# Attention within a tile: the causal mask taken from TensorE and given to VectorE and GpSimd

## The reference

```python
def fox_block(q, k, v, Fq, Fk, qpos, kpos):
    s = einsum('bqhd,bkhd->bhqk', q, k) * FOX_HEAD_DIM ** -0.5
    s = s + (Fq[..., :, None] - Fk[..., None, :])          # forget gate, moved to (head, query, key)
    s = where(kpos[None, :] <= qpos[:, None], s, -inf)
    p = softmax(s, axis=-1)
    return einsum('bhqk,bkhd->bqhd', p, v)
```

## Time and profile before

| what | value |
|---|---|
| median of 3 runs | 3674.41 us (3671.79 to 3679.04) |
| the profiled execution | 3677.2 us, span of its trace 3675.5 us |
| PE busy | 3058.5 us, 83% |
| DVE busy | 2164.2 us, 59% |
| ACT busy | 1057.2 us, 29% |
| POOL busy | 1440.1 us, 39% |
| mean granted clock of TensorE | 0.963 of 2.4 GHz |
| first block | up to about 850 us |

### The profile page before, as it was taken

The page is one execution under the profiler, slowest core; times in us unless marked ns, Lnnn a source line. Parts: engine busy times, 40 slices in busy tenths (PEclk is TensorE's granted clock), DMA queues, the critical chain, the costliest instruction groups (busy, mean ns, idle before and its releaser), DMA issues.

```text
span 3675.5 us, 29378 instructions
## 1 busy us (share of the span) xinstructions
PE 3058.5 (83%) x9023; PEld 1415.7 (39%) x9023; DVE 2164.2 (59%) x5158; ACT 1057.2 (29%) x3284; POOL 1440.1 (39%) x1185
## 2 busy tenths in 40 slices
PE   6899999997768977987897788788878878887776
PEld 2566666665213333332332333233333333332222
DVE  0343444434885775686577558657855865785444
ACT  1122222223323233223322322332232233223222
POOL 0000000001444555555555454545545554555553
PEclk7789999999879999999999999999999999999999
DMA  9300000032999999999999999999999999999998
GB/s 342 126 20 30 29 23 21 21 118 98 422 373 422 421 421 418 421 421 416 416 421 416 412 422 414 418 421 417 416 410 422 421 416 412 421 419 421 421 418 349
DMA packets 196495, 1219.15 MB, mean 332 GB/s; under 512 B 35696, under 2 KB 36656, under 8 KB 55792
## 3 DMA queue, kind: packets, MB, share of 16 engines
q0 software_dynamic: 156672, 1140.92, 75.1%
q1 hardware_dynamic: 39664, 76.34, 5.8%
HBM read 1205.68 MB, written 11.50 MB: 331 GB/s over the span
## 4 chain that ended last, share of the span: by engine, by line
DMA 45%; PE 8%; DVE 8%; issue 7%; ACT 5%; POOL 4%; POOLq 0%
DMA shared<-in_uv,eidx_even 23%; DMA shared<-in_uv,eidx_odd 22%; PE bank L942 8%; DVE shared L1244 5%; POOL shared L907 4%; ACT wt L1042 2%; ACT dg L1046 2%; ACT ge L1039 1%; PE bank L954 0%; DVE ti L1127 0%; DVE shared L1162 0%; DVE shared L1159 0%; DVE shared L1129 0%; DVE bp L1127 0%; DVE e L1164 0%
## 5 line engine op out<-in xcount | busy, mean ns | idle before, releaser
L942 PE MATMUL bank<-shared,dg 128*128 128x512 f32 (+1 forms) x4352 | 2002.8, 623 | 527.9 <-ACT dg L1046 527.8
L942 PEld LDWEIGHTS bank<-shared,dg 128*128 128x128 f32 (+1 forms) x4352 | 768.4, 191 | 1753.7 <-ACT dg L1046 952.4
L907 POOL DMA_INDIRECT shared<-in_uv,eidx_even x576 | 738.4, 1282 | 769.9 <-PE bank L942 638.0
L1244 DVE CUSTOM_DVE_ANT_0 shared<-shared,h_even 128x1024 f32<-128x1024 f32 x576 | 702.1, 1222 | 502.3 <-DMA shared<-in_uv,eidx_even 501.2
L907 POOL DMA_INDIRECT shared<-in_uv,eidx_odd x512 | 654.8, 1279 | 638.1 <-PE bank L942 554.7
L1244 DVE CUSTOM_DVE_ANT_0 shared<-shared,h_odd 128x1024 f32<-128x1024 f32 x512 | 625.2, 1222 | 420.8 <-DMA shared<-in_uv,eidx_odd 419.7
L1039 ACT ACTIVATE ge<-dots 128x2 f32<-128x2 f32 x544 | 110.6, 203 | 1878.3 <-DVE dots L1244 1878.2
L1046 ACT ACTIVATE dg<-ident,wt 128x128 f32<-128x128 f32 x1024 | 355.3, 394 | 16.7
L929 PE MATMUL bank<-wk,h2T 128*128 128x512 f32 x512 | 260.5, 595 | 0.0
L370 PE MATMUL bank<-shared,hT 128*128 128x512 f32 (+3 forms) x576 | 221.5, 546 | 0.0
L283 POOL TENSOR_SCALAR qr<-qs 128x8 f32<-128x8 f32 (+1 forms) x9 | 1.8, 196 | 409.7 <-DVE qs L695 409.7
(11 more groups left out here) (286 smaller groups left out, 2051.3 us busy)
## 6 DMA issues: line engine op xcount, KB each, us to landing
wout<-in_w_ada SPq DMA_DIRECT2D x12, 2048.0 KB, 9.0
shared<-in_w_in SPq DMA_DIRECT2D x1, 10288.0 KB, 33.2
shared<-in_uv,eidx_even POOLq DMA_INDIRECT x576, 12.5
shared<-in_uv,eidx_odd POOLq DMA_INDIRECT x512, 12.5
wout<-in_w_out SPq DMA_DIRECT2D x1, 4096.0 KB, 31.3
xn<-in_x_prompt SPq DMA_DIRECT2D x8, 512.0 KB, 5.4
xt<-in_x_prompt SPq DMA_DIRECT2D x8, 512.0 KB, 4.7
xmid<-mix SPq DMA_DIRECT2D x8, 512.0 KB, 3.1
```

The lines of the kernel that those rows point to most:

```text
L907: pool.indirect_dma_start(ring[:, k % RING, :], None, a["uv"], bass.IndirectOffsetOnAxis(flat(eidxs[n % 2][:, :, :])[:, k:k + 1], 0)).then ...
L942: mm = pe.matmul(bank[SUM_BANK(n) + c][at:at + T, :], dg[:, k % RING, 0:T], ring[:, k % RING, DM + 512 * c:DM + 512 * c + 512], start=(k = ...
L1244: ins = dve.tensor_tensor_reduce(ring[:, sl, 0:DM], ring[:, sl, 0:DM], h2s[n % 2][:, :], 1.0, 0.0, ALU.mult, ALU.add, dots[:, k:k + 1])
```

## The change

The two mask matmuls go. For the maximum, DVE adds `maskq` to the own scores of all four heads in one tensor_tensor into the first half of `mix`, and reduces from there. Since `mix` is written earlier in the tile than before, DVE waits there for the store of the last tile's xmid. For the weights, the exponential is taken of unmasked own scores, and GpSimd sets the entries with key > query to zero in place (`affine_select`), once per head, after the exponential and before PE's weighting with the own keys. PE waits for that with a new semaphore `own_masked`. GpSimd's queue is now: power for q and k, power for v, select of head 0, of head 1, power for the next x, select of head 2, power for y, select of head 3.

```diff
--- before.py
+++ after.py
@@ -177,6 +177,7 @@
             HB = lambda n: (HIST(n) + 3) // 4
             HIST_BEFORE = lambda n: sum(FH * HB(m) for m in range(n))
             KEYS_BEFORE = lambda n: sum(FH * (HB(m) + 1) for m in range(n))
+            own_probs = lambda h, T: (pT[0:T, 8, 0:T], pown[0:T, 0:T])[h % 2]
             KEY_BANK = lambda n, h, c: 5 + h % 3 if HB(n) == 0 else 6 - c if HB(n) == 1 else 5 + (c + 1) % 3
 
             @block.sync
@@ -283,14 +284,26 @@
                     then(pool.tensor_scalar(out, src, 1.0 / mean_of, EPS, ALU.mult, ALU.add))
                     pool.tensor_tensor(out, out, mhalf[0:out.shape[0], 0:out.shape[1]], ALU.pow).then_inc(sem(done), 1)
 
+                def own_masked(n, h):
+
+
+                    T = T_OF(n)
+                    pool.wait_ge(sem("pT_exp"), KEYS_BEFORE(n) + (HB(n) + 1) * (h + 1))
+                    pool.affine_select(out=own_probs(h, T), in_=own_probs(h, T), pattern=[[1, T]], compare_op=ALU.is_ge, fill=0.0,
+                                       base=0, channel_multiplier=-1).then_inc(sem("own_masked"), 1)
+
                 power(rstd[0:TS, :], ssum[0:TS, :], DM, "x_sq", 0, "rstd")
                 for n in range(NT + 1):
                     T = T_OF(n)
                     power(qr[0:T, :], qs[0:T, :], FD, "qk_sum", n, "qk_rstd")
                     power(vr[0:T, :], var[0:T, :], 64, "v_var", n, "v_rstd")
+                    own_masked(n, 0)
+                    own_masked(n, 1)
                     if n < NT:
                         power(rstd[:, :], ssum[:, :], DM, "x_sq", n + 1, "rstd")
+                    own_masked(n, 2)
                     power(yr[0:T, :], ysum[0:T, :], SI, "y_sq", n, "y_rstd")
+                    own_masked(n, 3)
 
             @block.tensor
             def _(pe):
@@ -403,8 +416,7 @@
                     if not FIRST(n):
                         pe.wait_ge(sem("hist_kept"), n)
                     for h in range(FH):
-                        pe.matmul(bank[2][0:T, h * P:h * P + T], qT[0:AUG, h, 0:T], kc[0:AUG, h, 0:T], start=True, stop=False)
-                        mm = pe.matmul(bank[2][0:T, h * P:h * P + T], ident[0:T, 0:T], maskq[0:T, 0:T], start=False, stop=True)
+                        mm = pe.matmul(bank[2][0:T, h * P:h * P + T], qT[0:AUG, h, 0:T], kc[0:AUG, h, 0:T], start=True, stop=True)
                     mm.then_inc(sem("own_scores"), 1)
                     pe.wait_ge(sem("um_gelu"), n + 1)
                     pe.wait_ge(sem("sums_used"), n + 1)
@@ -445,8 +457,7 @@
                                     mm = pe.matmul(bank[bk][:, j * P:j * P + T], kh[0:AUG, h, (4 * c + j) * P:(4 * c + j + 1) * P], qT[0:AUG, h, 0:T],
                                                    start=True, stop=True)
                             else:
-                                pe.matmul(bank[bk][0:T, 0:T], kc[0:AUG, h, 0:T], qT[0:AUG, h, 0:T], start=True, stop=False)
-                                mm = pe.matmul(bank[bk][0:T, 0:T], maskq[0:T, 0:T], ident[0:T, 0:T], start=False, stop=True)
+                                mm = pe.matmul(bank[bk][0:T, 0:T], kc[0:AUG, h, 0:T], qT[0:AUG, h, 0:T], start=True, stop=True)
                             mm.then_inc(sem("key_scores"), 1)
 
                     def weigh(h):
@@ -454,6 +465,7 @@
                         probs, own = ((pT, pT[:, 8, :]), (pT2, pown))[h % 2]
                         for j in range(HT):
                             pe.matmul(bank[2][0:T, h * 65:h * 65 + 65], probs[:, j, 0:T], vh[:, j, h, :], start=(j == 0), stop=False)
+                        pe.wait_ge(sem("own_masked"), n * FH + h + 1)
                         pe.matmul(bank[2][0:T, h * 65:h * 65 + 65], own[0:T, 0:T], vt[0:T, h, :], start=(HT == 0), stop=True).then_inc(sem("pv"), 1)
 
                     by_key(0)
@@ -571,7 +583,7 @@
                                 w = min(4, HT - 4 * c)
                                 ins = act.activation((pT, pT2)[h % 2][:, 4 * c:4 * c + w, 0:T], bank[bk][:, :].rearrange("p (j n) -> p j n", j=4)[:, 0:w, 0:T], ACT.Exp)
                             else:
-                                ins = act.activation((pT[0:T, 8, 0:T], pown[0:T, 0:T])[h % 2], bank[bk][0:T, 0:T], ACT.Exp)
+                                ins = act.activation(own_probs(h, T), bank[bk][0:T, 0:T], ACT.Exp)
                             ins.then_inc(sem("pT_exp"), 1)
                         if h == 1 and not last:
                             act.wait_ge(sem("x_in"), 16 * n + 32)
@@ -729,7 +741,10 @@
                     ins.then_inc(sem("M"), 1)
 
                     dve.wait_ge(sem("own_scores"), n + 1)
-                    then(dve.tensor_reduce(mh[0:T, :, 0], bank[2][0:T, :].rearrange("p (h n) -> p h n", h=FH)[:, :, 0:T], X, ALU.max))
+                    prev(dve, sem("xmid_stored"), n * 16)
+                    own4 = mix[0:T, 0:512].rearrange("p (h n) -> p h n", h=FH)[:, :, 0:T]
+                    then(dve.tensor_tensor(own4, bank[2][0:T, :].rearrange("p (h n) -> p h n", h=FH)[:, :, 0:T], bc(maskq[0:T, 0:T].rearrange("p (h n) -> p h n", h=1), [T, FH, T]), ALU.add))
+                    then(dve.tensor_reduce(mh[0:T, :, 0], own4, X, ALU.max))
                     for h in range(FH):
                         for c in range(HB(n)):
                             i = h * HB(n) + c
```

## The result

The changed kernel takes 3696.76 us (median of 5, 3691.31 to 3699.35) against 3674.41 us before (3671.79 to 3679.04): ratio 1.0055, 95% interval 1.0043 to 1.0068. It is slower by 0.55% (22 us between the medians, 20 between the profiled executions), and outside the forecast range. The profiled execution took 3697.26 us with a span of 3695.5 us.

The account below looks back on a forecast made before the run. The second block's gathers end last, so only its start, set by the first block, can move. Tile 0 -2.5, tile 1 +0.1, tiles 2 and 3 +1.5, tiles 4 to 8 +0.3: -0.6 us, giving 3673.8 us, range 3667 to 3682.

Parts of the forecast that it names:

- What bounds the kernel: Second block's gathers end last, untouched; the change moves only the first block, where DVE is late at the own scores.
- The add: Own scores, tiles 2 to 8: DVE's mask add costs 0.72 us per tile on the path, +5.0 us in all.
- PE would be 0.9 us earlier, but only waits longer for DVE: worth nothing.: Own scores, tiles 2 to 8: removing four PE mask pairs (0.9 us) gains nothing, since DVE is late.
- vanish in that wait: net 0: Own scores, tile 1: removed masks vanish in PE's 0.75 us wait for DVE's products; the add has room; net 0.
- Tile 0: First tile, partly at the 1.2 GHz level: own masks -1.3 us, by-key masks -1.2 us, together -2.5 us.
- By key, tiles 4 to 8: Scores by key: three exposed mask pairs leave PE's path, -0.66 us per tile, -3.3 in all; GpSimd's select is covered.
- Tiles 1 to 3, priced at nothing: Scores by key: the removed 0.66 us runs into PE's wait for vn, worth 0; later vn adds +0.2 us in all.
- the row of the power operation: GpSimd's power on 128x4 did not stretch beside DVE, so no contention was priced; by the contention rule about +1 us instead.
- Rival (a): GpSimd becomes the late one, with selects up to 1.65 us: +8.7 us, 3682 us in all; chance 0.06.
- Rival (c): Tile 0's clock shifts because PE's passes change: 3664 or 3684 us; chance 0.08, half to each side.
- Either sign: Clock shifts from changed PE passes could gain or lose: 10 us for 20 us of PE work at the other level.

Follow-up runs that it names:

- kernel with four pairs: Whole change plus four mask-sized matmul pairs per tile that compute nothing, behind the own scores; against the kernel before: 3669.05 us, ratio 0.9992.
- without own masks: Kernel before with PE's four own-score masks left out and nothing in their place (maximum over unmasked scores): 3690.79 us, ratio 1.0043.
- the add alone: Kernel before with DVE's mask add put in and all PE masks kept: 3684.09 us, ratio 1.0025.
- own-score half: Kernel before with DVE adding the own-score mask instead of PE; scores by key still masked by PE, no GpSimd select: 3699.39 us, ratio 1.0066.
- G: Theory, not a run: PE's wider waits between own scores and scan products make its granted clock fall behind them, and that is the loss.
- by-key half alone: Kernel before with only the GpSimd select replacing PE's masks by key; own scores masked by PE, no DVE add: 3669.32 us, ratio 0.9985.
- changed kernel with the gap filled: Whole change plus six idle matmul pairs behind the second history score, in tiles with history; against the kernel before: 3677.44 us, ratio 1.0006.
- the one with both places filled: Whole change plus idle matmul pairs behind the own scores and behind history scores; against the kernel before: 3668.19 us, ratio 0.9983.
- filled by-key half: Kernel before with only the by-key masks moved to GpSimd, plus one to four idle matmul pairs at PE's other waits: 3672.51 us, ratio 0.9992.

## Why the prediction was wrong

**What bounds the kernel** was read rightly: only the first block moved, and DVE, not PE, was the late one at the own scores.

**The add** was right at +0.72 us and on the path (11.12 against 10.40 us in tile 5 of the kernel with four pairs). Its row came out at 0.68 us for a forecast 0.67 to 0.69.

**"PE would be 0.9 us earlier, but only waits longer for DVE: worth nothing."** This is the step that failed. The wait was seen, and sized, and priced at zero because PE is not the late engine there. At a held clock the price of zero was right (10.40 us in tile 5 with the masks and without). But a PE that waits wasn't free here: the clock that it got afterwards went with the wait, and what stands behind the wait (later history scores, scan products) is on the path. The removed masks and the added DVE work both widened the same wait, from 0.9 to 2.5 us in tile 2 and from nothing to 1.7 us in tile 5. The masks' removal alone costs 16 us (without own masks), the add alone 10 us (5 of it its own term), both together 24 us (own-score half). Each is mostly the clock.

**Tile 1's masks "vanish in that wait: net 0"** failed in the same way. Its wait for the products grew from 0.75 us to 1.64, and the clock fell; the tile grew by 1.9 us. In all five profiled kernels with a wait of 1.64 to 1.68 us there the clock falls during it or within 2 us of its end, in none of the eight with 0.75 us or less.

**Tile 0** was -5.8 us for -2.5, and the profiles of the halves part it. From the mark to the first scores by key it took 12.77 us before and 9.54 after, -3.2 for a forecast of -1.3. All six profiled kernels whose PE masks the own scores take 12.7 to 12.9 us there and have a fall that begins 0.7 to 1.6 us behind the mark; six of the seven others take 8.8 to 9.5 without it, the seventh 10.4 with one. From there to the mark of tile 1 it is 74.8 us in all five kernels with the masks by key and 72.2 to 72.3 in seven of the eight without, -2.6 for a forecast of -1.2. Before the change, then after it:

```profile
170.50:177.00 6.50, 6.50 (x14) 2.31 (x14) 2.58 (x6) 0.00 (x0) 0.00 (x0) 0.50 0.00 0
...
166.50:177.00 10.50, 8.68 (x46) 4.07 (x44) 9.34 (x21) 0.63 (x2) 1.20 (x2) 1.00 0.00 1
```

The sum mis-sized both terms because it took the low clock as given. With the clock held the own masks are worth nothing there too: the kernel with four pairs takes the same 9.54 us. Why the early fall goes with the masks isn't shown, and G doesn't explain it: the change widens PE's wait there from nothing to 1.33 us, and the clock gets better.

**By key, tiles 4 to 8** was right: -0.67 in tile 5. In tile 8 it was more, 14.40 for 15.23 us, since there the first mask pair was exposed as well. Tiles 1 to 3, priced at nothing, were shorter by 0.1 to 0.2 us each in the kernel with four pairs. The by-key half alone was to bring 4.3 us and brought some 5.5 (0.9985). It may have a price of its own: of the seven profiled kernels that have this half and no pairs in front of the wait for vn, five lose the clock in tile 2 at the scores by key or behind them, some 2.6 us each where it could be compared; of the five that mask by key on PE, none does. No run was made to test that.

**GpSimd.** The select took 0.29 us as forecast where nothing else was going on, but not always: over the profiled execution it had a median of 292 ns and a maximum of 785 (ns min/median/max, then first and last start):

```profile
L292 POOL TENSOR_SCALAR_AFFINE_SELECT pown<-pown x18: 232/292/785, 179.9 to 841.1; 128x128 f32<-128x128 f32 x16, 64x64 f32<-64x64 f32 x2
...
340.48 0.44 PE L469 MATMUL bank<-vt,pown 128*128 128x65 f32 x2 [0.51 <-POOL pown L292]
```

All ten above 0.31 us in this execution overlap DVE instructions on SBUF, as the 0.57 us one overlaps L633 above. Not every such overlap stretched one: the select at 573.21 took 0.29 us beside a product of two SBUF tensors. The prediction held the row of the power operation against the rule of the Trainium skill (GPSIMD Engine Reference, "Key points") that GpSimd contends with DVE for SBUF; here the stretched selects agree with the rule and the row misled, probably since that operation hardly reads anything. It cost little: PE waited for a select four times, all in tiles 1 and 2, 1.8 us together (0.60 us the longest), and PE waits for vn behind it anyway. Rival (a) did not come about; in the by-key half alone its whole price is inside a gain.

**Rival (c)** named the clock, gave it 0.08, and looked for it in tile 0, where it had been low already. I read the clock where it had fallen, and not the waits behind which it might fall next. "Either sign" was the other fault: in tiles 1 to 8 the change widens PE's waits in front of the scan products and narrows none of them, and there every difference of the clock was a loss. The gain that it also allowed came in tile 0 alone. The rows for this were at hand: L732 back to back behind L728 says that each microsecond taken from PE becomes waiting.

**The range**, 3667 to 3682, was made of the sum's bounds and the run-to-run spread; the mechanism that gave the result wasn't among the terms. Rival (c)'s upper price, 3684, was worked out for 20 us of PE work at the lower level; the six falls in tiles 2 to 7 hold 51 us.

## What to carry to other kernels

Where PE waits for another engine, work taken from PE in front of the wait isn't free and can cost more than it was: add up all of PE's waits in the stretch before and after the change, and if they grow, price the matmuls behind them at the lower clock level as a case of its own, not as noise. Check it by putting matmuls that compute nothing into the wait; if the kernel gets faster, it is the clock. And try the halves of a change apart: here one gains 0.15% and the other loses 0.66%.

## What the runs showed of the hardware

The granted clock fell to 0.5 behind waits that look harmless. In the changed kernel PE waited 1.66 to 2.54 us in tiles 2 to 7 and each wait was followed by a stretch of 7 to 14 us at about half clock; in tile 8 it waited 1.88 us and nothing happened. Waits of 1.1 to 1.6 us were followed by a fall in some tiles and some executions and not in others, which is why two kernels had executions on two levels, 3679 and 3689 us for the one with the add, and 3669 and 3685 to 3691 us for the one with four pairs. What a fall needs can't be said from these runs beyond the count under the table. At the scores by key four falls came behind waits of 0.69 us and less (tile 2 in the by-key half, in the changed kernel with the gap filled and in the one with both places filled; tile 5 in the filled by-key half). In tiles 0 and 1 the clock falls at the scores by key in every kernel, the one before included. The Trainium skill (TensorE: Matmul & The Clock Gate, "HAM oscillation — how this bites in real kernels") describes a kernel whose PE loses its clock time after time at its waits for DMA; here the waits were for VectorE and shorter, and the pattern, one fall per tile, is the same in tiles 2 to 7 of the changed kernel.

A GpSimd select of 128x128 that takes 0.29 us alone took up to 0.79 us beside DVE work on SBUF.
